# The opening of a two-block kernel: first weights in halves on ScalarE's queue, products of zeros ahead, constants in two parts, and a bank for the fifth tile

## The chip, the cores and the metric

The kernel runs on one core of a Trainium2 chip. The metric is the device time of one execution in microseconds: 1484.77 us as the median of three runs (1482.9 to 1485.26).

A core has TensorE for matrix products, VectorE (DVE), ScalarE (ACT) and GpSimd (POOL) for elementwise work, and SyncE, which here only issues transfers. Each engine runs its own instructions in order, and they wait for each other through semaphores.

## The reference

The reference computes two transformer blocks one after the other on x of 512 tokens by 1024 features, in float32. The first one's mixer is a linear recurrence (RWKV-7) beside a cross attention to 256 memory tokens; the change touches its beginning alone:

```python
kv = rms_norm(mem, mem_norm_g) @ w_mem_kv
h = rms_norm(x, norm_mix_g)
proj = h @ w_in                       # 1024 -> 2816 features
slab = token_shift(proj[..., :2560], mu)   # z + (z_prev - z) * mu
q_mem = proj[..., 2560:]
r, k, v, wd, ad, gd = split(slab)
log_w = -softplus(-(w0 + tanh(wd) @ w2)) - 0.5
a = sigmoid(a0 + ad @ a2)
g = sigmoid(gd) @ g2
...                                   # delta rule over 512 steps, 12 heads
x = x + concat([mix, mem_out]) @ w_out
x = x + square(relu(rms_norm(x) @ w_ff1)) @ w_ff2
# second block: neighbourhood and sliding window attention, gated; then a SwiGLU
```

## The kernel before

Activations lie with features on the partitions, so a product of weights and x gives a tile of 128 features by 512 tokens. Float32 accuracy is had from three fast products: a weight matrix and x are each split into a high part (`Whi`, `Hhi`: rounded to the fast format by ScalarE) and a low part (`Wlo`, `Hlo`: the remainder, subtracted by VectorE), and a *block* of 128 input features is Whi·Hhi, Wlo·Hhi, Whi·Hlo (`mm3`, called from L1089's `mm`). A tile of eight blocks is therefore 24 products of 128x512.

Weights come in *units* of 128x1024 (512 KB), one unit for one tile. SyncE loads a unit into one of three sets (`Wraw`, set 0 to 2, and set 3 once), ScalarE casts it (`split` in the scalar program, L2135), VectorE subtracts (L1685). A set may be overwritten by the next cast only when the tile that used it has ended (`of_unit`), so ScalarE waits for TensorE there.

`make_plan` writes one list of steps. Each engine walks through it and takes the steps that are its own, so a step's place in the list is its place on every engine. In the beginning the list brings x in eight pieces of 128 features (`xload`, `x`), and four tiles grow side by side, one block each per piece (`firsts`: wa, gd and two slabs, on units 0 to 3, sets 0 to 3). The norm of x is applied after the product. For its factor ScalarE squares and sums the rows of x (`row`, four of 128 tokens, L2150), takes the root (L2167), VectorE inverts it and spreads it (L1719, L1722, into `acc`), TensorE turns it by a transposing product (`rs`, L1203), and VectorE copies it to `RS` (L1732). Only then can VectorE read the four tiles out of their banks (L1742), after which ScalarE and VectorE do the token shift (L2200, L1819). Next come the fifth tile (unit 4, set 0), the two small products of the decay and rate (on `WA`, `w2s`), and the two tiles of memory queries (units 5 and 6, sets 1 and 2), then the memory projections (x 256 columns).

Accumulators are eight banks: two that tiles take in turn (`D`), five handed out round robin (`M`, where a tile may have its `own`), and one more (`OB`). Constants (`C`, 1794 columns) come in one transfer, needed first for the root's epsilon and the identity of the transposes.

## Time and profile before

| | |
|---|---|
| median of three runs | 1484.77 us |
| the profiled execution, its own time | 1485.25 us |
| its span, first to last instruction | 1483.5 us |
| TensorE, products busy | 1446.6 us, 98% |
| VectorE busy | 794.9 us, 54% |
| ScalarE busy | 555.4 us, 37% |
| GpSimd busy | 225.9 us, 15% |
| mean rate of transfers | 88 GB/s (331 in the first fortieth of the span) |

The span lies 1.75 us under the execution's own time. Busy shares are means over the span; matrix products are pipelined, and the ends of the rows are modelled, so the distance between starts says more than the duration that a row gives. "Idle before" in brackets is how long the engine had nothing, with what ended that.

### The profile page before, as it was taken

To read this page: it belongs to the slowest core of one execution; us is meant where nothing else is said; L and a number is where in the kernel's file an instruction comes from. 1 tells how busy PE (TensorE), PEld (TensorE's weight loads), DVE (VectorE), ACT (ScalarE), POOL (GpSimd) and SP (SyncE) were. 2 spreads that over 40 slices of the span, in tenths; PEclk is the share of its full clock that TensorE was granted. 3 is DMA by queue.
4 is the path that set the end of the run, shared out by engine and by line. 5 is a ranking of instruction groups with operands and counts; after the bars stand their busy time and mean duration, and the time that the engine had idled before them with its cause. 6 is when DMAs were issued, how large, how long until landed. Compare 5 with 4: busy or idle time off the path is not lost.

```text
span 1483.5 us, 26651 instructions
## 1 busy us (share of the span) xinstructions
PE 1446.6 (98%) x11374; PEld 1157.1 (78%) x11374; DVE 794.9 (54%) x1266; ACT 555.4 (37%) x942; POOL 225.9 (15%) x161
## 2 busy tenths in 40 slices
PE   7999999989999999999999999999999999999999
PEld 6877777666888888888888866767788888888887
DVE  5665676764563544536643457587554443443343
ACT  6544534552422221212532356555343222232221
POOL 0233333301200000000110001322112210220120
PEclk9999999999999999999999999999999999999999
DMA  8311111201323233332222232221232332333222
GB/s 331 114 30 46 31 31 45 74 3 59 99 86 102 97 100 93 106 93 92 94 91 86 81 111 79 89 68 58 86 99 93 101 104 87 100 97 103 85 86 99
DMA packets 39334, 130.89 MB, mean 88 GB/s; under 512 B 4272, under 2 KB 5296, under 8 KB 39216
## 3 DMA queue, kind: packets, MB, share of 16 engines
q1 hardware_dynamic: 39216, 129.18, 27.3%
q8 instruction: 90, 1.47, 0.4%
q14 instruction: 28, 0.23, 0.0%
HBM read 127.07 MB, written 2.10 MB: 87 GB/s over the span
## 4 chain that ended last, share of the span: by engine, by line
PE 87%; DVE 4%; issue 2%; ACT 2%; POOLq 0%; POOL 0%; DVEq 0%; ACTq 0%
PE bank L1089 85%; PE bank L1489 1%; PE bank L1203 1%; DVE slab L1819 0%; ACT kbr L2382 0%; ACT slab L2351 0%; DVE T L1924 0%; ACT Whi L2135 0%; PE bank L1279 0%; DVE Wlo L1685 0%; PE bank L1446 0%; DVE AR L1869 0%; DVE AR L1865 0%; DVE Xi L1931 0%; DVE ta L1868 0%
## 5 line engine op out<-in xcount | busy, mean ns | idle before, releaser
L1089 PE MATMUL bank<-Hhi,Whi 128*128 128x512 f32 x912 | 371.2, 407 | 8.7 <-DVE Wlo L1685 8.1
L1089 PE MATMUL bank<-Hlo,Whi 128*128 128x512 f32 x912 | 357.5, 392 | 0.0
L1089 PE MATMUL bank<-Hhi,Wlo 128*128 128x512 f32 x912 | 357.4, 392 | 0.0
L2135 ACT CAST Whi<-Wraw 128x1024 fp32r<-128x1024 f32 (+1 forms) x216 | 223.8, 1037 | 197.2 <-PE bank L1089 194.8
L1685 DVE TENSOR_TENSOR Wlo<-Wraw,Whi 128x1024 fp32r<-128x1024 f32 (+1 forms) x180 | 230.4, 1280 | 123.3 <-ACT Whi L2135 123.2
L1089 PE MATMUL bank<-Uhi,Whi 128*128 128x512 f32 x736 | 289.3, 393 | 1.6 <-DVE tmpb L1788 1.3
L1089 PE MATMUL bank<-Ulo,Whi 128*128 128x512 f32 x736 | 286.5, 389 | 0.0
L1089 PE MATMUL bank<-Uhi,Wlo 128*128 128x512 f32 x736 | 286.5, 389 | 0.0
L1089 PEld LDWEIGHTS bank<-Hhi,Whi 128*128 128x128 f32 x912 | 172.1, 189 | 56.8 <-issue 12.6
L1089 PEld LDWEIGHTS bank<-Hlo,Whi 128*128 128x128 f32 x912 | 172.2, 189 | 37.2
L1089 PEld LDWEIGHTS bank<-Hhi,Wlo 128*128 128x128 f32 x912 | 172.5, 189 | 33.0 <-issue 1.2
L1089 PEld LDWEIGHTS bank<-Uhi,Whi 128*128 128x128 f32 x736 | 138.1, 188 | 34.9 <-issue 3.8
L1089 PEld LDWEIGHTS bank<-Ulo,Whi 128*128 128x128 f32 x736 | 138.2, 188 | 28.9
L1089 PEld LDWEIGHTS bank<-Uhi,Wlo 128*128 128x128 f32 x736 | 138.2, 188 | 28.0 <-issue 0.2
L2463 POOL TENSOR_TENSOR Wlo<-Wraw,Whi 128x1024 fp32r<-128x1024 f32 x36 | 86.1, 2390 | 332.2 <-ACT Whi L2135 331.5
L1767 DVE TENSOR_TENSOR X<-X,bank 128x512 f32<-128x512 f32 x72 | 49.4, 686 | 138.2 <-PE bank L1089 138.1
L2471 POOL TENSOR_TENSOR accb<-accb,tmpb 128x512 f32<-128x512 f32 x14 | 18.9, 1352 | 375.9 <-ACT tmpb L2250 375.9
L2210 ACT CAST Uhi<-tmpb 128x512 fp32r<-128x512 f32 x32 | 19.9, 622 | 127.5 <-DVE tmpb L1776 127.5
L2476 POOL TENSOR_TENSOR qa<-qa 128x512 f32<-128x512 f32 x22 | 28.4, 1293 | 196.4 <-ACT qa L2220 196.4
L2224 ACT CAST Hhi<-qa 128x512 fp32r<-128x512 f32 x22 | 13.7, 622 | 114.6 <-POOL qa L2481 114.6
L2392 ACT ACTIVATE sr<-sr,st 128x256 f32<-128x256 f32 (+1 forms) x64 | 33.7, 528 | 34.7 <-DVE st L2060 20.4
L2077 DVE COPY pT<-bank 128x512 f32<-128x512 f32 (+2 forms) x48 | 25.3, 554 | 34.2 <-PE bank L1489 34.2
(292 smaller groups left out, 1556.4 us busy)
## 6 DMA issues: line engine op xcount, KB each, us to landing
Wraw<-in_wts SPq DMA_DIRECT2D x208, 512.0 KB, 3.5
bA<-in_biasA SPq DMA_DIRECT2D x12, 256.0 KB, 2.7
Wraw<-in_wts SPq DMA_DIRECT2D x8, 384.0 KB, 3.1
x<-in_xT SPq DMA_DIRECT2D x8, 256.0 KB, 4.5
x_rows<-in_xN SPq DMA_DIRECT2D x2, 1024.0 KB, 8.1
X<-in_xT SPq DMA_DIRECT2D x2, 1024.0 KB, 6.6
out<-X SPq DMA_DIRECT2D x8, 256.0 KB, 2.0
bB<-in_biasB SPq DMA_DIRECT2D x4, 384.0 KB, 3.0
```

Source lines behind the costliest of these rows:

```text
L1089: return e.matmul(o, lhsT, rhs, start=start, stop=stop, skip_group_check=True)
L1203: p = e.transpose(b[:, 128 * j:128 * j + 128], sq[:, 128 * j:128 * j + 128], c("ident"))
L1489: p = e.transpose(o, sr[n % 3][:, x:x + 128], c("ident"))
L1685: e.tensor_tensor(Wsp[k][1][:, 0:width], Wraw[k][:, 0:width], Wsp[k][0][:, 0:width].bitcast(F), ALU.subtract).then_inc(S["wlo"])
L1767: e.tensor_tensor(y, y, z, ALU.add).then_inc(S["evict"])
L2077: e.tensor_copy(pT[n % 2][:, width * i:width * i + wide], MB[plan.M.at["at", n, i]][:, 0:wide]).then_inc(S["at_out"])
L2135: e.copy(Wsp[k][0][:, 0:width], Wraw[k][:, 0:width]).then_inc(S["whi"])
L2210: e.copy(Uhi[:, x.key[1], :], tmp_of(("raw", t))[:]).then_inc(S["ffhi"])
L2392: p = e.activation(part, part, ACT.Exp, scale=1.0, bias=x[:, 2 + i:3 + i], accum_out=x[:, 4 + i:5 + i])
L2463: done(e.tensor_tensor(Wsp[k][1][:, 0:width], Wraw[k][:, 0:width], Wsp[k][0][:, 0:width].bitcast(F), ALU.subtract), "wlo_pool")
L2471: done(e.tensor_tensor(accb[:], accb[:], tmp_of(("sqr", *x.key))[:], ALU.add), "sq_add")
L2476: done(e.tensor_tensor(z[:], z[:], s[:], ALU.mult), "sig")
```

## The change

It touches the beginning alone; from the memory projections on, all engines have the same instructions in the same order as before.

- Unit 0's load leaves SyncE's queue. ScalarE issues it in two halves of 512 columns as its first instructions, casts each half by itself, and VectorE subtracts each half by itself.
- The very first block waits for its operands one by one and is written in the order Whi·Hhi, Whi·Hlo, Wlo·Hhi.
- VectorE sets a buffer (`km`) to zero, and TensorE multiplies it by itself four times (float32, 256 columns) ahead of everything.
- The constants come in two transfers (528 and 1280 columns with 14 of padding), later than before; the memory's second half is loaded, cast and split later.
- The fifth tile has its own bank. Its first four blocks stand ahead of the turning of the norm's rows. Unit 4 is loaded and cast earlier in the list: ahead of the last two row squares.
- Some semaphores are merged, and counts shifted by one.

On ScalarE, between the memory's splits and the load of the table for tanh, the rows were these (`x_rows` are the row squares, `st` the root, `Whi_62` the cast into set 0, `memHhi` the memory's high parts):

```order
L2156 ACTIVATE memHhi<-memX,V 128x256 [waits s_mem1]
L2156 ACTIVATE memHhi<-memX,V 128x256 x3
L2150 ACTIVATE x_rows,mst<-x_rows 128x1024 [waits s_xrows0]
L2150 ACTIVATE x_rows,mst<-x_rows 128x1024
L2150 ACTIVATE x_rows,mst<-x_rows 128x1024 [waits s_xrows1]
L2150 ACTIVATE x_rows,mst<-x_rows 128x1024
L2255 ACTIVATE spare<-C 128x1 [waits s_C]
L2167 ACTIVATE st_53<-mst,C 128x8 [waits s_xrow]
L2135 CAST Whi_62<-Wraw_59 128x1024 [waits s_tile,s_win0]
L2255 ACT_TABLE_LOAD
```

and they are now:

```order
L2212 ACTIVATE x_rows,mst<-x_rows 128x1024 [waits s_xrows0]
L2212 ACTIVATE x_rows,mst<-x_rows 128x1024
L2197 CAST Whi_62<-Wraw_59 128x1024 [waits s_tile,s_win0]
L2212 ACTIVATE x_rows,mst<-x_rows 128x1024 [waits s_xrows1]
L2212 ACTIVATE x_rows,mst<-x_rows 128x1024
L2317 ACTIVATE spare<-C 128x1 [waits s_C]
L2229 ACTIVATE st_53<-mst,C 128x8 [waits s_row]
L2218 ACTIVATE memHhi<-memX,V 128x256 [waits s_mem1]
L2218 ACTIVATE memHhi<-memX,V 128x256 x3
L2317 ACT_TABLE_LOAD
```

The cast, which waits for a tile to end, has moved ahead of two row squares and of the root; four of the memory's splits have moved behind it.

On TensorE, where the side-by-side tiles end (bank 2 and 3 are the two slabs, `C,acc` the turning of the norm's rows), there stood:

```order
L1089 MATMUL bank2<-Hhi_55,Wlo2_67 128x512
L1089 MATMUL bank2<-Hlo_56,Whi2_66 128x512
L1203 MATMUL bank4<-C_49,acc_100 128x128 [waits s_wide]
L1203 MATMUL bank4<-C_49,acc_100 128x128 x3
L1089 MATMUL bank3<-Hhi_55,Whi3_127 128x512
L1089 MATMUL bank3<-Hhi_55,Wlo3_128 128x512
```

and now, with the twelve products of the fifth tile's first four blocks shown by their first three:

```order
L1102 MATMUL bank3<-Hhi_55,Wlo3_128 128x512
L1102 MATMUL bank3<-Hlo_56,Whi3_127 128x512
L1102 MATMUL bank4<-Hhi_55,Whi0_62 128x512 [waits s_wlo]
L1102 MATMUL bank4<-Hhi_55,Wlo0_63 128x512
L1102 MATMUL bank4<-Hlo_56,Whi0_62 128x512
...
L1239 MATMUL bank5<-C_49,acc_100 128x128 [waits s_wide]
L1239 MATMUL bank5<-C_49,acc_100 128x128 x3
L1102 MATMUL bank3<-Hhi_55,Whi3_127 128x512
```

The turning moved behind four blocks of the fifth tile, which wait for unit 4's split. The diff, without the hunks that only rename or recount semaphores:

```diff
--- before
+++ after
@@ -20,6 +20,8 @@
 LEVELS = (1, 2, 4, 8, 16, 32)
+WARM = 4
+AHEAD = 2
 DECAY = 0.6065306597126334
@@ -28,9 +30,9 @@
 
-CONSTS = [("bd64", 128), ("mean", 128), ("ident", 128), ("cent", 128),
+CONSTS = [("bd64", 128), ("mean", 128), ("ident", 128), ("cent", 128), ("rmseps", 1), ("gneps", 1), ("pad", 14),
           ("mneg", 64), ("mpos", 64), ("inclneg", 64), ("inclpos", 64),
-          ("level", 64 * 5), ("first", 64), ("firstt", 64), ("same", 64), ("scan", 512), ("rmseps", 1), ("gneps", 1)]
+          ("level", 64 * 5), ("first", 64), ("firstt", 64), ("same", 64), ("scan", 512)]
 VECS = [("gmem", 8), ("gmix", 8), ("gffn", 8), ("mu", 20), ("w0", 6), ("a0", 6), ("kk", 6),
...
@@ -392,26 +395,36 @@
 
-        if i == 1:
-            step("cload")
-        elif i in (2, 3):
-            step("memload", i - 2)
+        if i == 2:
+            step("memload", 0)
         if i == 3:
-            for j in range(2):
-                step("rowload", "x", j)
+            step("rowload", "x", 0)
+            loads(5)
+            step("rowload", "x", 1)
+            step("cload", 0)
+            step("memload", 1)
             loads(6)
+            step("cload", 1)
             step("gateload")
         if i == 7:
-            for j in range(8):
+            for j in range(4):
                 mem_token(j)
-            for j in range(4):
+            for j in range(2):
+                step("row", "x", j)
+            splits(5)
+            for j in range(2, 4):
                 step("row", "x", j)
             next(first_norm)
+            for j in range(4, 8):
+                mem_token(j)
 
         for g, n in zip(firsts, ((1, 0, 0, 0), (1, 2, 2, 0), (1, 1, 1, 0))[i] if i < 3 else (1, 1, 1, i < 7)):
             for _ in range(n):
                 next(g)
-    splits(5)
+    first_values = couples(tile("slab", (0, 2), ("rw", 12), "x", range(8), own=True))
+    next(firsts[3])
+    for _ in range(AHEAD):
+        next(first_values)
     run(first_norm)
@@ -593,8 +606,8 @@
     def values_and_queries():
-        v = projection(0, 2)
-        yield from itertools.islice(v, 4)
+        v = first_values
+        yield from itertools.islice(v, 4 - AHEAD)
         t = read_out(v)
...
@@ -1122,10 +1135,33 @@
 
+        def first_block():
+
+            whi, wlo = Wsp[0]
+            o = bank_of(0)[:, 0:T]
+            w.wait_ge(S["whi"], 1)
+            w.wait_ge(S["xhi"], 1)
+            mm(o, whi[:, 0:128], Hhi1[:, 0, :], True, False)
+            w.wait_ge(S["Hlo"], 1)
+            mm(o, whi[:, 0:128], Hlo[:, 0, :], False, False)
+            w.wait_ge(S["wlo"], 1)
+            mm(o, wlo[:, 0:128], Hhi1[:, 0, :], False, False)
+
+        def warm_up():
+
+            w.wait_ge(S["setup"], 1)
+            for i in range(WARM):
+                mm(OB[:, 0:256], km[:, 0, 0:128], km[:, 1, :], True, True)
+
         def weight_block(t, i):
+            if t == 0 and i == 0:
+                first_block()
+                return
             x = tiles[t]
             hi, lo = acts(x.ver)
-            if i == 0:
+            if x.unit == 0:
+                w.wait_ge(S["wlo"], 1 if i < 4 else 2)
+            elif i == 0:
                 w.wait_ge(*lo_of(x.unit))
...
@@ -1306,6 +1342,7 @@
         def turn_a(p):
+            w.wait_ge(S["C_rest"], 16)
             crossed("na", (p,), 64, lambda h, ch, half: AR[p % 2][64 * h:64 * h + 64, 0, 64 * ch:64 * ch + 64],
...
@@ -1532,6 +1569,7 @@
                  "mv": mem_values, "as": scores, "at": turn_weights, "av": weighted, "vbt": turn_vb}
+        warm_up()
         for kind, *key in plan.steps:
@@ -1665,6 +1703,7 @@
         def setup():
+            e.memset(km[:], 0.0).then_inc(S["setup"])
             w.wait_ge(S["V"], 16)
@@ -1676,10 +1715,22 @@
 
+        def first_split():
+
+            raw, hi, lo = Wraw[0], Wsp[0][0], Wsp[0][1]
+            w.wait_ge(S["whi"], 1)
+            e.tensor_tensor(lo[:, 0:512], raw[:, 0:512], hi[:, 0:512].bitcast(F), ALU.subtract).then_inc(S["wlo"])
+            w.wait_ge(S["whi"], 2)
+            e.tensor_tensor(lo[:, 512:1024], raw[:, 512:1024], hi[:, 512:1024].bitcast(F),
+                            ALU.subtract).then_inc(S["wlo"])
+
         def split(u):
+            if u == 0:
+                first_split()
+                return
             lo, n = lo_of(u)
             if plan.numbers[("lo", u)] == "wlo":
-                w.wait_ge(S["whi"], u + 1)
+                w.wait_ge(S["whi"], u + 2)
                 width = units[u][1]
...
@@ -2123,7 +2175,17 @@
 
+        def first_split():
+
+            w.wait_ge(S["win_a"], 16)
+            e.copy(Wsp[0][0][:, 0:512], Wraw[0][:, 0:512]).then_inc(S["whi"])
+            w.wait_ge(S["win0"], 16)
+            e.copy(Wsp[0][0][:, 512:1024], Wraw[0][:, 512:1024]).then_inc(S["whi"])
+
         def split(u):
+            if u == 0:
+                first_split()
+                return
             k, before = sets.at[u], sets.before[u]
...
@@ -2420,6 +2482,12 @@
 
+        def first_unit():
+
+            e.dma_start(Wraw[0][:, 0:512], wts[0, :, 0:512]).then_inc(S["win_a"], 16)
+            e.dma_start(Wraw[0][:, 512:1024], wts[0, :, 512:1024]).then_inc(S["win0"], 16)
+
+        first_unit()
         w.wait_ge(S["zero"], 1)
...
@@ -2558,7 +2626,8 @@
             width = units[u][1]
-            e.dma_start(Wraw[k][:, 0:width], wts[u, :, 0:width]).then_inc(S[f"win{k}"], 16)
+            if u:
+                e.dma_start(Wraw[k][:, 0:width], wts[u, :, 0:width]).then_inc(S[f"win{k}"], 16)
 
@@ -2569,16 +2638,17 @@
 
-        def constants_in():
-            e.dma_start(C[:], cst).then_inc(S["C"], 16)
+        def constants_in(i):
+            a, z = ((0, C_FIRST), (C_FIRST, NCST))[i]
+            e.dma_start(C[:, a:z], cst[:, a:z]).then_inc(S[("C", "C_rest")[i]], 16)
 
         def mem_in(i):
             e.dma_start(memX[:, 4 * i:4 * i + 4, :],
                         memT[4 * i:4 * i + 4].rearrange("k p n -> p k n")).then_inc(S[f"mem{i}"], 16)
 
         def gates_in():
-            e.dma_start(w2s[:], w2a2).then_inc(S["w2"], 16)
-            e.dma_start(g2s[:], g2).then_inc(S["g2"], 16)
+            e.dma_start(w2s[:], w2a2).then_inc(S["w2g2"], 16)
+            e.dma_start(g2s[:], g2).then_inc(S["w2g2"], 16)
             e.dma_start(mem_rows[:], memN.rearrange("k p n -> p k n")).then_inc(S["memrows"], 16)
...
```

## Rows read from the trace of the kernel before

**Rows 1.** The page, the chain that ended last, by engine.

```profile
PE 87%; DVE 4%; issue 2%; ACT 2%; POOLq 0%; POOL 0%; DVEq 0%; ACTq 0%
```

**Rows 2.** Waits of TensorE, 0 to 66 us: total us, times, longest.

```profile
PE bank L1089 <- DVE Wlo L1685: 8.1, 1, 8.1
PE bank L1089 <- ACT x L2204: 0.9, 2, 0.6
```

**Rows 3.** Timeline of TensorE, opening: start, us, engine, line, operands, count.

```profile
8.07 0.79 PE L1089 MATMUL bank<-Hhi,Whi 128*128 128x512 f32 x1 [8.07 <-DVE Wlo L1685]
...
12.51 0.63 PE L1089 MATMUL bank<-Hhi,Wlo 128*128 128x512 f32 x1
12.94 0.45 PE L1089 MATMUL bank<-Hlo,Whi 128*128 128x512 f32 x1
...
13.70 0.39 PE L1089 MATMUL bank<-Hlo,Whi 128*128 128x512 f32 x1
...
69.86 1.12 PE L1089 MATMUL bank<-ftmp,C 128*128 128x512 f32 x2
```

**Rows 4.** Windows: stretch, busy by engine (x), granted clock, DMA share, GB/s.

```profile
2.00:3.00 1.00, 0.00 (x0) 0.00 (x0) 0.48 (x7) 0.23 (x2) 0.00 (x0) 1.00 0.67 138
3.00:4.00 1.00, 0.00 (x0) 0.00 (x0) 0.18 (x3) 0.01 (x1) 0.00 (x0) 1.00 1.22 334
...
8.10:10.00 1.90, 1.90 (x5) 1.51 (x6) 1.22 (x2) 1.53 (x2) 0.00 (x0) 1.00 1.02 399
```

**Rows 5.** Timeline of ScalarE, opening to 37 us.

```profile
4.00 0.72 ACT L2141 ACTIVATE Hhi<-x,V 128x512 fp32r<-128x512 f32 x1 [1.75 <-DMA x<-in_xT]
...
8.28 1.05 ACT L2135 CAST Whi<-Wraw 128x1024 fp32r<-128x1024 f32 x1 [0.90 <-DMA Wraw<-in_wts]
...
25.97 1.04 ACT L2150 ACTIVATE x_rows<-x_rows 128x1024 f32<-128x1024 f32 x1
...
27.01 0.19 ACT L2255 ACTIVATE spare<-C 128x1 f32<-128x1 f32 x1
...
28.48 1.05 ACT L2135 CAST Whi<-Wraw 128x1024 fp32r<-128x1024 f32 x1 [1.04 <-PE bank L1089]
...
36.65 1.03 ACT L2135 CAST Whi<-Wraw 128x1024 fp32r<-128x1024 f32 x1
```

**Rows 6.** Timeline of VectorE, opening to 38 us.

```profile
6.79 1.23 DVE L1685 TENSOR_TENSOR Wlo<-Wraw,Whi 128x1024 fp32r<-128x1024 f32 x1 [1.29 <-ACT Whi L2135]
...
9.36 2.45 DVE L1685 TENSOR_TENSOR Wlo<-Wraw,Whi 128x1024 fp32r<-128x1024 f32 x2 [0.68 <-ACT Whi L2135]
...
19.79 3.25 DVE L1696 SCALAR_TENSOR_TENSOR memHlo<-memX,V,memHhi 128x256 fp32r<-128x256 f32 x8
...
27.70 0.43 DVE L1722 COPY acc<-st 128x512 f32<-128x512 f32 x1
...
30.70 0.68 DVE L1732 COPY RS<-bank 128x512 f32<-128x512 f32 x1
...
37.71 1.23 DVE L1685 TENSOR_TENSOR Wlo<-Wraw,Whi 128x1024 fp32r<-128x1024 f32 x1 [1.07 <-ACT Whi L2135]
```

**Rows 7.** Timeline of TensorE, 28 to 54 us.

```profile
28.00 0.39 PE L1089 MATMUL bank<-Hlo,Whi 128*128 128x512 f32 x1
...
29.59 0.60 PE L1203 MATMUL bank<-C,acc 128*128 128x128 f32 x4
...
36.94 1.13 PE L1089 MATMUL bank<-WA,w2s 64*128 64x512 f32 x4
...
39.48 0.40 PE L1089 MATMUL bank<-Hhi,Whi 128*128 128x512 f32 x1
...
50.68 1.16 PE L1089 MATMUL bank<-C,x 128*128 128x128 f32 x8 [0.59 <-ACT x L2204]
...
53.50 0.28 PE L1089 MATMUL bank<-memHhi,Whi 128*128 128x256 f32 x1
```

**Rows 8.** Timeline of SyncE, opening: the issue of the first weights.

```profile
1.63 0.42 SPq L2561 DMA_DIRECT2D Wraw<-in_wts  x1
```

More of the change, by code:

```diff
@@ L47 @@
 C_AT, NCST = offsets(CONSTS)
+C_FIRST = C_AT["mneg"][0]
 V_AT, NVEC = offsets(VECS)
@@ L958, in block_program @@
     assert top[0] <= nc.sbuf_usable_end, top[0]
-    old, old_end = (C_AT_BYTES + 4 * C_AT[n][0] for n in ("mneg", "rmseps"))
+    old, old_end = (C_AT_BYTES + 4 * n for n in (C_FIRST, NCST))
     sr.append(sb_at("sr2", [128, 768], F, old))
@@ L998, in block_program @@
     S = {n: nc.alloc_semaphore("s_" + n) for n in (
-        "V C w2 g2 mem0 mem1 memrows xrows0 xrows1 X0 X1 xin0 xin1 xin2 xin3 win0 win1 win2 win3 win4 bias0 bias1 bias2 out "
+        "V C C_rest w2g2 win_a mem0 mem1 memrows xrows0 xrows1 X0 X1 xin0 xin1 xin2 xin3 win0 win1 win2 win3 win4 bias0 bias1 bias2 out "
         "whi wlo wlo_pool Hlo Ulo mlo umem memhi mixhi ffhi bothhi uphi uhi "
@@ L1009, in block_program @@
         "ms_out mt_out va_act va_dve as_out at_out vbt_out "
-        "setup zero gd dve wide xhi xrow mrow mhi hsq lora shift_a shift sgp tap cum kf0 exp pc kksq bt rk ar bb "
+        "setup zero gd dve wide xhi row mhi hsq lora shift_a shift sgp tap cum kf0 exp pc kksq bt rk ar bb "
         "bk x0 y0 ai zsq bonus mmax mrec pn hkb amax aexp arec an sqr gated gact gsig sig act resq "
@@ L1082, in lo_of @@
         kind = plan.numbers[("lo", u)]
-        return S[kind], N(kind, u)
+        return S[kind], N(kind, u) + (kind == "wlo")
     def tensor_program(e):
@@ L1219, in decay @@
         def decay(p):
-            w.wait_ge(S["w2"], 16)
+            w.wait_ge(S["w2g2"], 32)
             w.wait_ge(S["lora"], 1)
@@ L1426, in gate_rows @@
         def gate_rows(p):
-            w.wait_ge(S["g2"], 16)
+            w.wait_ge(S["w2g2"], 32)
             w.wait_ge(S["gd"], 1)
@@ L1835, in cumulate @@
             w.wait_ge(S["sgp"], p + 1)
+            w.wait_ge(S["C_rest"], 16)
             e.tensor_tensor_scan(sg[:], c("scan"), sg[:], 0.0, ALU.mult, ALU.add).then_inc(S["cum"])
@@ L1990, in head_rows @@
             w.wait_ge(S["hn"], N("hn", t))
-            w.wait_ge(S["setup"], 1)
+            w.wait_ge(S["setup"], 2)
             if x.kind == "km":
@@ L2150, in row_squares @@
             e.activation(rows_, rows_, ACT.Square, scale=1.0,
-                         accum_out=row_sums[name][:, j:j + 1]).then_inc(S[name + "row"])
+                         accum_out=row_sums[name][:, j:j + 1]).then_inc(S["row"])
         def mem_token(i):
@@ L2164, in root @@
             if kind in ("x", "m"):
-                w.wait_ge(S[kind + "row"], n // 128)
+                w.wait_ge(S["row"], 4 if kind == "x" else 6)
                 one = row_sums[kind].unsqueeze(2).broadcast_to([128, n // 128, 2])
@@ L2189, in evict @@
                 dst, z, j = shifted(t)
-                w.wait_ge(S["setup"], 1)
+                w.wait_ge(S["setup"], 2)
                 if x.kind == "slab" and x.key[0]:
@@ L2260, in decay @@
             w.wait_ge(S["sg"], p + 1)
-            w.wait_ge(S["setup"], 1)
+            w.wait_ge(S["setup"], 2)
             e.activation(sg[:], MB[plan.M.at["sg", p]][:], ACT.Tanh, scale=0.5,
@@ L2275, in keys @@
             w.wait_ge(S["tap"], p + 1)
-            w.wait_ge(S["setup"], 1)
+            w.wait_ge(S["setup"], 2)
             w.wait_ge(S["sk"], p)
@@ L2459, in split @@
             if plan.numbers[("lo", u)] == "wlo_pool":
-                w.wait_ge(S["whi"], u + 1)
+                w.wait_ge(S["whi"], u + 2)
                 turn()
```

## Prediction, before the changed kernel was run

> **What bounds the kernel now.** I read the page first: the chain of waits that ends last is TensorE's for 87% [rows 1]. A change elsewhere counts only where it shortens or lengthens a TensorE wait. So the second view was TensorE's waits up to 66 us. The two longest entries are 8.1 us before its first product, for the low half of the first weights, and 0.9 us in two waits for ScalarE [rows 2]. From 8.07 us to 49.7 us it never stands still. Third came the timelines of the opening, and last the same timelines at 28 to 40 us, where the change reorders work.
>
> [...] First, the first product starts at 8.07 us. [...] The engine had stood still for 8.07 us before, and then worked without a pause for 4.9 us until the spacing fell. The granted clock of the windows reads 1.00 even there [rows 4], so it is the spacing that tells the level.
>
> **The change part by part.** I go in four steps: start of the dense stream, the chain that it releases, the stretch after, and the edits that cost nothing.
>
> *Step 1, the start.* The first weights leave SyncE's queue for ScalarE's, in halves, and the first block needs only the high halves to begin. ScalarE's high half of x took 0.72 us from 4.00 [rows 5]; a 512-wide cast is about half of the 1.05 us of a 1024-wide one [rows 5], 0.55; so the first product may start near 5.4 us instead of 8.07. But the order then wants the second weight tile after six products, and its path is not shortened by any edit except the transfer: landing at 8.28 (the cast starts there, and its wait ends on the transfer), split at 9.36 and 1.28 us from the split's start to the product, as 6.79 to 8.07 at the first tile [rows 3, 5, 6]. That is 8.28 + 1.08 + 1.28 = 10.64. What matters is how much earlier that transfer lands. The core moved 138 GB/s from 2 to 3 us and 334 from 3 to 4, against 399 later [rows 4]: only the first 3 us are not full. Two queues issuing at once can fill at most about (399 - 138) + (399 - 334) = 326 KB of that, 0.8 us at 399; the least is nothing, if the two share what one had. I take 0.5 (nearer to the filled end, since SyncE also issues everything behind the first weights one slot earlier). So the dense stream starts at 10.14 us.
>
> The products of zeros: the trace has no such product that cold. The nearest row is the fp32 product of 128x512, two passes in 1.12 us at the fast level (69.86) [rows 3]; 256 columns are half, 0.56, and at the slow level 1.12; four are 2.2 to 4.5 us. The zeroing memset needs well under 1 us, so they lie between about 1.3 and 5.8 us, where the engine stood still: free, or up to 0.4 us off the first block, which has 10.14 - 5.8 us to spare. What they may buy is the fast level at 10.14.
>
> If it is fast: the tile that frees weight set 0 ends 71 products after the dense stream's first. At 0.227 us that is 16.1 us, so its last product starts at 26.26 instead of 28.00 [rows 3, 7]. The opening's gain at this point is G = 1.74 us.
>
> *Step 2, the chain that is released.* Write c for the moment at which ScalarE casts the fifth unit's weights (set 0): 28.48 before, 0.48 behind that last product [rows 5, 7], so 26.74 now. Before, the sums of squares of x were all done by then (27.01), TensorE turned their rows at 29.59 and VectorE copied them at 30.70, that is c + 2.22 [rows 5 to 7]. Now the cast stands ahead of two of the four row squares, and TensorE takes four blocks of the fifth tile ahead of the turning. ScalarE's side: cast 1.05, two squares of 1.04, and 1.12 from the small step at 27.01 to the end of VectorE's spread copy at 28.13 give c + 4.3 [rows 5, 6]. TensorE's side: the fifth tile's split is ready at c + 1.08 + 1.28 = c + 2.36 (three blocks after the freeing tile are over at c + 1.8, so it waits 0.6), four blocks are 12 x 0.227 = 2.72, and the turned rows are readable 0.60 to 1.11 later (29.59 x4 took 0.60; the copy at 30.70 is the upper end, as VectorE was still splitting). I take 0.66: c + 5.74. TensorE's side ends last, and VectorE's four memory splits that now stand ahead of the copy end a little sooner: the root is over at c + 3.5, then four high parts and the last low part at 0.41 each (3.25 for eight) make c + 5.5 [rows 6]. So the copy comes 5.74 - 2.22 = 3.52 us later against c, and 3.52 - 1.74 = 1.78 us later on the clock: 32.48.
>
> From the copy on, VectorE and ScalarE hand five evictions and shifts to each other in the old order. The cast of set 1 starts 5.95 after the copy (36.65) and its split 7.01 after (37.71) [rows 5, 6]; nothing in this stretch waited for TensorE, so it moves as a block. The split is then ready for TensorE at 32.48 + 7.01 + 1.28 = 40.77. TensorE gets there sooner: turning 0.36, nine and twelve products of 0.227, and 1.1 for the two small products (36.94, four passes) after c + 5.08 = 31.82 make 38.1 [rows 7]. It waits 2.7 us. Before it began set 1 at 39.48 with the split ready at 38.99: half a microsecond of cover, which is gone. Set 1 starts 40.77 - 39.48 = 1.29 us later than before. In general: 3.03 - G.
>
> *Step 3, from set 1 to the memory projections (53.50).* The same products stand here in a little other order. The trace has one wait of 0.59 in the stretch, at 50.68, for ScalarE [rows 7]. Now the key rows' turning stands last and waits for a table load and root that are queued behind more of ScalarE's casts. If TensorE is alone the limit, 0.6 is won; if ScalarE's queue is, up to 1 is lost. I take -0.1. From there on the order is the old one, and the lag stays: +1.2 us.
>
> *Edits at nothing.* Constants in two parts and the memory's second half later: both land in a stretch of full transfers some microseconds before their first use, and c + 3.1 (the first constant needed) is 29.8. If they were late, each microsecond would add one to the chain of step 2. The merged semaphores change no order. The own bank takes away a wait for an eviction that did not bind. The two DMA issues on ScalarE are 0.42 us each by SyncE's row [rows 8]; ScalarE stood idle for 1.75 us before x landed at 4.00 [rows 5], which covers both. If that cover were gone, the delay would still end before the second weights land.
>
> Sum against the profiled execution (span 1483.5, its own time 1485.25): +1.2 gives 1486.45. The median of the three runs is 1484.77, so by it 1485.97; I say 1486.0.
>
> **The rivals.**
>
> A. The gain stays. If set 1's split is ready when TensorE comes, the result is step 1 alone: -1.7 at G = 1.74 and -2.6 at most (transfer 0.8 earlier, first stretch 0.6 of step 3), so 1483.0. For it: the four blocks of the fifth tile are work put ahead of the turning, which is cover. Against it: TensorE's work up to set 1 has the same length as before, while the chain from the cast grew by 3.5. It needs 2.7 us that I do not see.
>
> B. The slow level is back when the dense stream starts. Between the first blocks and 10.14 TensorE has six products to do in over 4 us, and in step 2 it stands 2.7 us. A stretch like that of the trace, 11 products spaced 0.43 instead of 0.227 [rows 3], costs 2.2 us: G = -0.5, and the result is 3.03 + 0.5 - 0.1 = +3.4, 1488.2. It decides from 9 such products on (G below 0). [...]
>
> C. The second queue brings nothing: the transfers share the rate and the second weights land at 8.28 as before. Then G = 1.24 and the result +1.7, 1486.5. [...] The trace shows the rate short of full before 3 us, so there is room that a second queue can fill, and the forecast takes part of it.
>
> **How the numbers follow.** Forecast 0.50, A 0.15, B 0.22, C 0.13. Change of less than 0.2%, 3.0 us, is what a measurement here cannot tell from none: the three runs alone spread by 2.4. Forecast and C lie inside it; A passes it only with a good run (0.07 in all); B passes it most of the time (0.16, and 0.03 from the forecast's tail). So faster 0.07, same 0.74, slower 0.19. The range takes A's 1483 less a little scatter, and B's 1488.2 with some: 1482.8 to 1489.0. Forecast and C alone would be 1484.5 to 1487.5.
>
> **What would show it.** In the changed trace: first real product between 5.0 and 6.2 us; second weight tile's first product at 9.8 to 10.6, spaced 0.23 from there (0.43: rival B); the fifth unit's cast at 26.2 to 27.3; TensorE waiting about 0.6 us for that split; the copy of the turned rows at 32 to 33; and a wait of 2 to 3.5 us for set 1's split at about 38 us, which the old trace doesn't have. If that wait is under 0.5 us, step 2 is wrong; if it is there and the total still falls, G was mis-sized.

## Result and profile after

The changed kernel takes 1486.60 us as the median of 15 runs (1484.60 to 1489.32), the kernel before 1483.50 us on the same chip (15 runs, 1481.54 to 1485.66): a ratio of 1.0024, 95% interval 1.0017 to 1.0031. The medians are 3.1 us apart, and the interval is 2.5 to 4.6 us. The forecast was 1486.0, but as 1.2 above before. The median came close partly because the three runs of before that I started from were 1.3 us higher than fifteen are. The ratios here and below leave out one execution of 3644 us, of the kernel without zeros in the next section, whose median counts it. The profiled execution has a span of 1484.2 us and took 1486.00.

The chain of the page is still TensorE's for 87% [rows 1]:

```profile
PE 87%; DVE 5%; issue 2%; ACT 2%; POOLq 0%; POOL 0%; ACTq 0%; DVEq 0%
```

The waits of TensorE from 0 to 66 us (total us, times, longest), which answer to [rows 2]:

```profile
PE bank L1102 <- DVE Wlo L1736: 2.9, 2, 2.5
PE bank L1102 <- DVE km L1706: 1.5, 1, 1.5
PE bank L1102 <- ACT Whi L2181: 1.4, 1, 1.4
PE bank L1239 <- DVE VD L1768: 0.6, 1, 0.6
PE bank L1102 <- DVE Hlo L1742: 0.5, 1, 0.5
PE bank L1102 <- ACT x L2266: 0.2, 1, 0.2
```

The 8.1 us ahead of the first product are gone. In their place stand 1.5 before the zeros, 1.4 and 0.5 among the first blocks, and a new 2.5 for a low half of weights. Where that one is, the timeline of TensorE tells. First the opening, beside [rows 3] (start, us, engine, line, operands):

```profile
1.45 3.78 PE L1102 MATMUL bank<-km 128*128 128x256 f32 x8 [1.45 <-DVE km L1706]
6.60 0.80 PE L1102 MATMUL bank<-Hhi,Whi 128*128 128x512 f32 x1 [1.37 <-ACT Whi L2181]
...
8.75 0.80 PE L1102 MATMUL bank<-Hhi,Whi 128*128 128x512 f32 x1 [0.47 <-DVE Hlo L1742]
...
10.19 0.63 PE L1102 MATMUL bank<-Hhi,Whi 128*128 128x512 f32 x1
10.62 0.63 PE L1102 MATMUL bank<-Hhi,Wlo 128*128 128x512 f32 x1
...
13.18 0.49 PE L1102 MATMUL bank<-Hhi,Wlo 128*128 128x512 f32 x1
13.50 0.40 PE L1102 MATMUL bank<-Hlo,Whi 128*128 128x512 f32 x1
```

The second weight tile starts at 10.19, and its products are 0.43 us apart until 13.18. This spacing of 512-wide products is called the slow level here, and 0.227 us, measured before from 13.70 to 28.00 [rows 3, 7], the fast one. The slow level lasts about as long into the program as before, where it ended at 12.94. The same engine from 30 us on, beside [rows 7]:

```profile
30.67 0.50 PE L1102 MATMUL bank<-Hhi,Whi 128*128 128x512 f32 x1 [0.41 <-DVE Wlo L1736]
...
33.53 0.60 PE L1239 MATMUL bank<-C,acc 128*128 128x128 f32 x4
...
42.45 0.50 PE L1102 MATMUL bank<-Hhi,Whi 128*128 128x512 f32 x1 [2.47 <-DVE Wlo L1736]
...
56.21 0.63 PE L1239 MATMUL bank<-C,ftmp 128*128 128x128 f32 x4 [0.63 <-DVE VD L1768]
56.59 0.36 PE L1102 MATMUL bank<-memHhi,Whi 128*128 128x256 f32 x1
```

The turning (33.53) was at 29.59, set 1's first product (42.45) at 39.48, and the memory projections (56.59) began at 53.50: 2.97 us late, then 3.09. ScalarE, beside [rows 5]:

```profile
5.32 0.72 ACT L2203 ACTIVATE Hhi<-x,V 128x512 fp32r<-128x512 f32 x1 [2.15 <-DMA x<-in_xT]
...
28.31 1.05 ACT L2197 CAST Whi<-Wraw 128x1024 fp32r<-128x1024 f32 x1 [5.56 <-PE bank L1102]
...
40.12 1.03 ACT L2197 CAST Whi<-Wraw 128x1024 fp32r<-128x1024 f32 x1
```

VectorE in the same stretch, beside [rows 6]:

```profile
29.39 1.23 DVE L1736 TENSOR_TENSOR Wlo<-Wraw,Whi 128x1024 fp32r<-128x1024 f32 x1 [8.69 <-ACT Whi L2197]
...
32.05 0.43 DVE L1773 COPY acc<-st 128x512 f32<-128x512 f32 x1
32.40 1.67 DVE L1747 SCALAR_TENSOR_TENSOR memHlo<-memX,V,memHhi 128x256 fp32r<-128x256 f32 x4
34.17 0.69 DVE L1783 COPY RS<-bank 128x512 f32<-128x512 f32 x1
...
41.18 1.23 DVE L1736 TENSOR_TENSOR Wlo<-Wraw,Whi 128x1024 fp32r<-128x1024 f32 x1 [1.06 <-ACT Whi L2197]
```

The cast of the fifth unit (28.31) came 0.17 us sooner than before, the copy of the turned rows (34.17) 3.47 later. The transfers, by windows beside [rows 4] (the last number is GB/s):

```profile
2.00:3.00 1.00, 1.00 (x4) 0.78 (x3) 0.00 (x0) 0.99 (x2) 0.00 (x0) 1.00 0.80 186
3.00:4.00 1.00, 1.00 (x4) 0.82 (x3) 0.35 (x5) 0.16 (x1) 0.00 (x0) 1.00 0.95 320
```

The issue of the first half on ScalarE's queue, beside [rows 8]:

```profile
0.73 0.41 ACTq L2487 DMA_DIRECT2D Wraw<-in_wts  x1
```

From 2 to 3 us the core moved 186 GB/s where it had moved 138, and from 3 to 4 us 320 where it had moved 334; ScalarE issues the first half at 0.73, where SyncE had issued the whole at 1.63. The two halves landed at 3.99 and 5.48 (the whole at 5.69 before) and the second weights at 7.63 instead of 8.26. The vectors, however, landed at 3.62 instead of 2.49 and the first piece of x at 5.23 instead of 3.91.

### The profile page after: what moved, and what is told of

It reads as the page before. It is cut to its first block, busy times and chain, and to the rows that moved or that the text cites. A ratio compares the mean times of both kernels' runs of the same rounds, so it can differ in the third digit from the quotient of the medians.

```text
span 1484.2 us, 26671 instructions
## 1 busy us (share of the span) xinstructions
PE 1449.1 (98%) x11382; PEld 1157.5 (78%) x11382; DVE 795.1 (54%) x1268; ACT 555.1 (37%) x943; POOL 224.3 (15%) x161
## 4 chain that ended last, share of the span: by engine, by line
PE 87%; DVE 5%; issue 2%; ACT 2%; POOLq 0%; POOL 0%; ACTq 0%; DVEq 0%
PE bank L1102 85%; PE bank L1526 1%; PE bank L1239 0%; DVE slab L1870 0%; PE bank L1483 0%; ACT kbr L2444 0%; DVE T L1976 0%; ACT Whi L2197 0%; PE bank L1315 0%; DVE Wlo L1736 0%; DVE AR L1921 0%; DVE AR L1917 0%; DVE Xi L1983 0%; ACT slab L2413 0%; DVE ta L1920 0%
## 5 line engine op out<-in xcount | busy, mean ns | idle before, releaser
L2544 POOL TENSOR_TENSOR qa<-qa 128x512 f32<-128x512 f32 x22 | 28.5, 1294 | 196.8 <-ACT qa L2282 196.8
```

The lines of the kernel that those rows point to most:

```text
L2544: done(e.tensor_tensor(z[:], z[:], s[:], ALU.mult), "sig")
```

## Experiments

I call the lag of a kernel how much later than in the kernel before an instruction that both have starts. It is read between 60 and 290 us, since farther on the profiled executions differ by the stretches in which the granted clock fell (last section). Each kernel ran beside the kernel before, whose medians were 1483.35, 1483.16, 1483.12 and 1483.47 us in the four sessions.

**The order undone.** Steps for row squares, cast and fifth tile as before the change, its loads kept:

```diff
-            for j in range(4):
+            for j in range(8):
                 mem_token(j)
-            for j in range(2):
-                step("row", "x", j)
-            splits(5)
-            for j in range(2, 4):
+            for j in range(4):
                 step("row", "x", j)
             next(first_norm)
-            for j in range(4, 8):
-                mem_token(j)
...
-    for _ in range(AHEAD):
-        next(first_values)
+    splits(5)
```

> The changed kernel with its edits at the very start (halves, first block, zeros, constants in two parts) but with the old order of the row squares, the root, the fifth unit's cast and the fifth tile. Theory (the lag is the chain cast, split, four blocks, turning, copy): the copy of the turned rows comes 2.2 us behind the fifth unit's cast instead of 5.9, the first product on weight set 1 at about 39.3 us instead of 42.45, no wait of 2.5 us there, and the time 0.2 us under before, 3.3 us under the changed kernel. Rival (the lag comes from the later transfers of constants, memory and weights, or from the two queues): set 1 still begins at 42 us or later and the time stays about 3 us over before.

1487.86 us, ratio 1.0032 (1.0020 to 1.0044): a miss. It was no clean undoing. ScalarE now stood before all four row squares, waiting for the memory's second half, which the new order of loads brings later, in its timeline:

```profile
26.52 1.71 ACT L2210 ACTIVATE memHhi<-memX,V 128x256 fp32r<-128x256 f32 x4 [6.45 <-DMA memX<-in_memT]
```

So the root came late, and TensorE waited 3.4 us for it, in its timeline:

```profile
33.48 0.66 PE L1231 MATMUL bank<-C,acc 128*128 128x128 f32 x4 [3.38 <-DVE acc L1765]
```

The order of the loads and that of the steps belong together.

**The order alone**, put into the kernel before (the lines above the other way round, nothing of the start):

> The kernel before with nothing but the new order of row squares, root, fifth unit's cast and fifth tile. Theory: the start is that of before (first product at 8.07 us, cast at 28.5 us), the copy of the turned rows 5.8 us behind the cast, set 1 at 42.5 us, and the time 3.0 us over before. Rival (the new order is harmless, the lag belongs to the transfers or the start): set 1 at 39.5 us and the time of before.

1486.39 us, 1.0022 (1.0013 to 1.0031), as the theory had it. The cast came at 28.53, the copy of the rows at 34.39 (5.86 behind it), and set 1 waited:

```profile
42.68 0.50 PE L1098 MATMUL bank<-Hhi,Whi 128*128 128x512 f32 x1 [2.45 <-DVE Wlo L1694]
```

**The start alone**: the start's edits with the old order of steps and of loads.

```diff
-        if i == 2:
-            step("memload", 0)
+        if i == 1:
+            step("cload", 0)
+            step("cload", 1)
+        elif i in (2, 3):
+            step("memload", i - 2)
         if i == 3:
-            step("rowload", "x", 0)
-            loads(5)
-            step("rowload", "x", 1)
...
+            for j in range(2):
+                step("rowload", "x", j)
             loads(6)
```

> All of the start's edits (first weights in halves on ScalarE's queue, first block by operand, products of zeros, constants in two parts), with the order of the row squares, the cast, the fifth tile and of every later load as before the change. Theory (the start's edits are worth the 0.17 us that the cast of the fifth unit gained, and the whole loss is the new order's): first product 6.5, cast of the fifth unit at 28.2 to 28.4, copy of the turned rows 2.2 behind it (30.5), set 1 begins at 39.2 to 39.4 with no wait over 0.3 us for its split; time 0.1 to 0.3 us below the kernel before (1483.1 on a chip where before is 1483.35). It would also say that the 3.4 us wait of the first undoing came from its load order. Rival (the later landings of the first vectors and of x, from queues that now share, cost something of their own): set 1 over 1 us late, time 1 to 3 us above before.

1483.25 us, 1.0002 (0.9994 to 1.0011). Cast 28.61, copy 30.84, no wait for set 1, and up to 60 us no longer wait behind the first blocks than the 0.54 for the key rows (0.59 in before). The lag is +0.10 to +0.15 up to 200 us (0.3 to 0.4 at 245 to 280), not the small gain expected: in this execution the spacing fell only at 14.04. So the order is the loss (+3.0 between the medians), and the start is worth nothing, in trace and in time.

**No zeros** (`WARM = 0`), and **ones instead of zeros** (`e.memset(km[:], 1.0)`):

> The changed kernel without the four products of zeros. Theory (they bought nothing: the products after 6.6 us were spaced 0.43 us until 13.3 us all the same): the spacing falls to 0.23 us between 12 and 15 us again, set 1 begins within 0.5 us of 42.45, the time is that of the changed kernel within 0.5 us. Rival (they shortened the slow stretch that follows): the spacing falls 2 us later or more and the time grows by 1 us.

> The changed kernel with its four early products made of ones instead of zeros; nothing else. Theory A (what counts is that TensorE is busy, and four products in 1.45 to 5.23 us with the pause behind them are too little): the spacing falls at about 13 us as with zeros, same time. Theory B (zeros do not count as work): the spacing falls to 0.23 us well before 11 us, the fifth unit's cast comes 1 to 1.5 us sooner than 28.31, and the time is 1 to 1.5 us under the changed kernel.

1488.01 us, 1.0028 (1.0018 to 1.0038), and 1486.05 us, 1.0018 (1.0008 to 1.0028). With none, the slow spacing ended at 13.05; with four of ones at 13.98; with four of zeros at 13.2 in the changed kernel, and between 12.7 and 14.9 in the other kernels with four. Set 1 waited 2.45 and 2.48 us. The median without zeros is 1.4 us above the changed kernel's, where 0.5 was expected; the intervals overlap, and in the trace the lag is a little smaller (2.97 against 3.2 at 90 us). So no gain of the eight passes shows, and the values in them are not the reason.

**The cast back** behind all four squares and the root, the four blocks still ahead of the turning:

```diff
-            for j in range(2):
-                step("row", "x", j)
-            splits(5)
-            for j in range(2, 4):
+            for j in range(4):
                 step("row", "x", j)
             next(first_norm)
             for j in range(4, 8):
                 mem_token(j)
+            splits(5)
```

> The changed kernel, with the cast of the fifth unit back behind all four row squares, the root and the memory's last tokens; the four blocks of the fifth tile still stand ahead of the turning of the rows on TensorE. Theory (TensorE's side of the chain ends last: split, four blocks, turning, copy): the root is ready in time, and yet the copy comes 5.6 to 6.0 us behind the cast and set 1 waits 2.4 us or more; time 3 us or more above before. Rival (it was the cast among ScalarE's row squares that delayed the root): copy 2.2 behind the cast, no wait for set 1, time within 0.5 us of before.

1486.37 us, 1.0022 (1.0012 to 1.0032), as the theory had it. VectorE's spread copy was over at 27.75, yet TensorE turned it at 34.27, behind the four blocks:

```profile
34.27 0.60 PE L1237 MATMUL bank<-C,acc 128*128 128x128 f32 x4
...
43.19 0.50 PE L1100 MATMUL bank<-Hhi,Whi 128*128 128x512 f32 x1 [2.45 <-DVE Wlo L1734]
```

**No blocks ahead** (`AHEAD = 0`), the cast early as in the changed kernel:

> The changed kernel, with the cast of the fifth unit as early as in it, but no blocks of the fifth tile ahead of the turning (AHEAD 0). By the prediction's step 2, ScalarE's and VectorE's side then ends last: copy of the turned rows 4.3 to 5.2 us behind the cast instead of 5.86, so 0.7 to 1.5 us sooner; TensorE waits 2.0 to 3.5 us before the turning for the copied root, and then hardly at set 1; time 1.5 to 2.5 us above before. Rival (the four blocks are the whole loss): copy 2.2 to 3 behind the cast, time within 0.5 us of before.

1486.75 us, 1.0020 (1.0011 to 1.0030), that is 1.6 to 4.4 us above before where 1.5 to 2.5 was expected. TensorE waited for the root, as expected, and not at set 1; but the copy came at 33.63, 5.67 behind the cast (27.96), not 4.3 to 5.2. VectorE, with the fifth unit's split and the memory splits:

```profile
31.70 0.43 DVE L1773 COPY acc<-st 128x512 f32<-128x512 f32 x1
32.05 1.67 DVE L1747 SCALAR_TENSOR_TENSOR memHlo<-memX,V,memHhi 128x256 fp32r<-128x256 f32 x4
33.63 0.68 DVE L1783 COPY RS<-bank 128x512 f32<-128x512 f32 x1
```

The spread copy ended at c + 4.2, where step 2 had c + 4.3, and then the four memory splits stood before the copy: the c + 5.5 that step 2 gives for VectorE, which I forgot in this expectation. The two sides end 0.2 us apart, so taking off one of them gives nothing back.

**Ten products of zeros** in the changed kernel (`WARM = 10`), so that TensorE works up to its first block:

> The changed kernel with 10 products of zeros (20 passes) instead of 4, so that TensorE has no pause between them and the first block. Theory (the slow level stayed because TensorE stood still between the zeros and the dense stream, so my forecast's own condition wasn't met): the spacing falls to 0.227 before 9 us, the zeros end by 8.5 to 9.5, second weight tile's first product at 10.2 to 10.6 at the fast level, cast of the fifth unit at 26.6 to 27.2, set 1's wait about 2.4 as before, lag from set 1 on 1.3 to 2.0; time 1.3 to 1.8 us above before, so 1.3 to 1.8 below the changed kernel. Rival (the start's work doesn't set the level, or products of zeros don't count): spacing 0.43 until about 13, first product late at about 10, cast at 28.3 or later, time 3 us or more above before.

1486.31 us, 1.0020 (1.0011 to 1.0029). The trace did what was expected up to set 1. The zeros' spacing halved at 4.85 us and stayed so through the first blocks:

```profile
1.45 6.16 PE L1102 MATMUL bank<-km 128*128 128x256 f32 x20 [1.45 <-DVE km L1706]
...
10.44 0.50 PE L1102 MATMUL bank<-Hhi,Whi 128*128 128x512 f32 x1 [0.23 <-DVE Wlo L1736]
10.78 0.39 PE L1102 MATMUL bank<-Hhi,Wlo 128*128 128x512 f32 x1
```

VectorE's copy of the turned rows in the same kernel:

```profile
33.01 0.69 DVE L1783 COPY RS<-bank 128x512 f32<-128x512 f32 x1
```

And TensorE's first product of set 1 behind it:

```profile
41.30 0.50 PE L1102 MATMUL bank<-Hhi,Whi 128*128 128x512 f32 x1 [2.46 <-DVE Wlo L1736]
```

The cast came at 27.15, so G = 1.33; the copy 5.86 behind it; set 1 at 41.30, which is 1.82 behind before, where 3.03 - G gives 1.70. Behind that wait the clock fell (a window of 42.3 to 45.5; the column ahead of the DMA share is the granted clock), and the lag grew to 2.47:

```profile
42.30:45.50 3.20, 3.20 (x9) 2.45 (x9) 1.16 (x2) 2.76 (x5) 1.22 (x2) 0.50 0.45 159
```

The time doesn't show the gain: the interval (1.6 to 4.3 us above before) just touches what was expected (1.3 to 1.8) and holds the changed kernel's 3.1 too.

**The start with ten zeros** and the old order, **the kernel before with eleven zeros** and nothing else, and **one queue**, the first again with the halves issued by SyncE. The first and third change the start alone by the two lines shown; the second adds the memset, `warm_up` and `WARM = 11` to the kernel before; the third also moves the two issues:

```diff
-WARM = 4
+WARM = 10
...
-        first_unit()
...
+            else:
+                e.dma_start(Wraw[0][:, 0:512], wts[0, :, 0:512]).then_inc(S["win_a"], 16)
+                e.dma_start(Wraw[0][:, 512:1024], wts[0, :, 512:1024]).then_inc(S["win0"], 16)
```

> The start's edits with 10 products of zeros instead of 4, and the old order of the row squares, the cast, the fifth tile and the loads (the start alone, made to reach the fast level). Theory (by the trace of the changed kernel with 10 products of zeros the level rises at about 4.7 us and stays; the loss was the order's): second weight tile's first product at 10.2 to 10.6 spaced 0.227, cast of the fifth unit at 26.9 to 27.3, copy of the turned rows 2.2 behind it, set 1's split ready at copy + 8.28 = 37.4 to 37.8, TensorE there at 38.1 to 38.4, so no wait over 0.3 us; lag -1.1 to -1.4 from set 1 on, time 1.1 to 1.4 us below before, about 1481.9 where before is 1483.2. Rival (what is won at the start is given back later, by another wait or by the clock): lag at 120 us between -0.5 and +1, time within 0.6 us of before.

> The kernel before, with nothing added but the zeroing memset and 11 products of zeros ahead of its first product (no second queue, no halves, old order). Theory (the level is what the start can win, the earlier first product isn't): level up at about 4.7 us, zeros end by 7.9, first product at 8.1 spaced 0.227, a new wait of about 1 us for the second weights (ready at 10.64 by the old transfer), cast of the fifth unit at 27.0 to 27.3, lag -1.1 to -1.4 at 120 us, time 1.1 to 1.4 us below before. Rival (the level falls back in the wait for the second weights, or the second queue was needed): spacing 0.43 again behind 10.6, cast at 28 or later, time within 0.5 us of before.

> As the start with 10 products of zeros and the old order, but the two halves of the first weights are issued by SyncE, behind the vectors and the first token, so that all loads are in one queue again. Theory (the second queue takes its share from the vectors and from x, and gives the weights behind it what SyncE no longer issues): vectors landed at 2.5, first token at 3.9, halves at 4.8 and 5.7, second weights at 8.1 to 8.4 (7.5 to 7.8 with two queues); first product by the zeros' end at 7.2 to 7.3, second weight tile at 10.4 to 10.8, cast of the fifth unit within 0.3 us of the two queues'; time within 0.5 us of it. Rival (the second queue is needed): second weight tile and cast 0.6 us or more later.

1483.86 us, 1.0000 (0.9990 to 1.0009); 1481.50 us, 0.9994 (0.9986 to 1.0002); 1483.27 us, 1.0005 (0.9996 to 1.0014). In all three the fast level was there (from 5.87, 6.20 and 7.85 us) before the second weight tile (10.42, 10.67 and 11.03 us), and in none of the profiled executions did the gain stay: lags +0.1, +0.15 and +0.7. For the kernel before with zeros the times leave a small gain open: the interval runs from 2.1 us below before to 0.3 above. TensorE met a new wait at the turning. The kernel before with zeros, one line of TensorE's waits from 0 to 66 us:

```profile
PE bank L1210 <- DVE acc L1731: 0.9, 1, 0.9
```

Its third row square on ScalarE:

```profile
26.25 1.06 ACT L2159 ACTIVATE x_rows<-x_rows 128x1024 f32<-128x1024 f32 x1 [1.45 <-DMA x_rows<-in_xN]
```

And its transfers from 23 to 25 us (queue: packets, MB, share of 16 engines):

```profile
q1 hardware_dynamic: 223, 0.80, 99.6%
q8 instruction: 1, 0.02, 3.0%
```

The squares of x's last rows begin when those rows have landed: at 26.25 here, at 24.91 in before, where the spread copy (28.13) stood ready 1.46 us before TensorE turned it [rows 6, 7]. That was all the cover there was, and two things together used it up: TensorE came 1.1 sooner, and the rows came 1.3 later. By these rows the 1.1 alone would have fitted into the cover. In this kernel a piece of instructions (16 KB, one packet of 1.0 us on one transfer engine, at 23.61) was loaded among the rows, whose second half landed 3.6 us behind the first instead of 2.5; in before that packet came at 33.85, in the changed kernel at 28.15. With one queue (packet at 24.43) the halves also landed 3.6 apart. In the start with ten zeros both landed 1.7 later than in the start with four, and only 2.55 apart, with the packet (23.89) behind the first half's landing (23.61), so there the packet can't be the cause, and what is stays open. That the packet delays the rows is read from these rows, not tested.

One queue also settled what the second one does: vectors at 2.60 and first piece of x at 3.97 as in before, second weights at 8.64, against 8.03 with two. The second weight tile came 0.6 later, and so did the cast, as the rival said.

**Rows first**, to remove that bound: the changed kernel's loads, ten zeros, old order, and the memory's last four tokens behind the cast of set 1.

```diff
     splits(6)
     shift(held[3])
+    for j in range(4, 8):
+        mem_token(j)
```

> The changed kernel with 10 products of zeros, its own order of loads (x's rows ahead of the memory's second half), but the cast of the fifth unit behind the four row squares and the root, no blocks of the fifth tile ahead, and the memory's last four tokens only behind the cast of set 1. Theory (the start's gain was lost twice: with the old loads the rows of x land too late for an earlier turning, 24.5 to 26.2 us, and with the new order the cast and the four blocks stand ahead of it; with the rows first and the old order nothing is in its way): level up at 4.7 to 5.9 us, second weight tile at 10.2 to 10.5, row squares over by 26.8, cast of the fifth unit at 27.0 to 27.4, copy of the turned rows at 29.2 to 29.7, set 1's first product at 38.1 to 38.5 with no wait over 0.3 us, lag -1.0 to -1.3 at 120 us, time 1.0 to 1.3 us below before (1482.1 where before is 1483.1). Rival (the moved tokens or another wait take it back): a wait of over 0.5 us between 28 and 60 us that before does not have, lag at 120 us between -0.5 and +2, time not below before.

1485.20 us, 1.0006 (0.9997 to 1.0015): a miss. The rows landed at 26.0 again (packet at 23.87), TensorE waited 0.94 at the turning and reached set 1 at 39.30, only 0.18 sooner than before (38.1 to 38.5 was expected). Then the key rows came late; that the four tokens, which now stand in the queues of ScalarE and VectorE, are the reason is read from the order, not tested:

```profile
39.30 0.40 PE L1096 MATMUL bank<-Hhi,Whi 128*128 128x512 f32 x1
...
52.21 1.45 PE L1096 MATMUL bank<-C,x 128*128 128x128 f32 x8 [2.31 <-ACT x L2260]
```

By that wait the profiled execution was 1.5 us behind before, and behind it the granted clock was 0.50 from 53 to 56.3 us, so that its lag is 2.9 from 66 us on, above both expectations. The interval of the times is 0.4 below before to 2.2 above.

No version here is shown to beat the kernel before.

## Why the prediction was right, and which size was off

The sign, the place and the range held; the forecast itself did not come about by its own sum. What came about is rival B, and that 1486.0 lies only 0.6 below the median is luck: G was 1.57 short, and the start of the sum was 1.3 too high.

*Step 1, the start: the step that failed.* The forecast took the fast level at 10.14 us and G = 1.74. The transfer term came out in size: the second weights landed 0.63 sooner (0.5 taken), and their first product came at 10.19. Its reason did not: from 2 to 4 us, the stretch that was to be filled, the core moved 506 KB where it had moved 472, which is worth about 0.1 us at 399 GB/s by my estimate. What the rest comes from stays open, and so does part of the size: with the start of before the second weights landed at 7.84 to 8.29 in three kernels, with the second queue at 7.41 to 8.03 in ten. But the first real product came at 6.60, not near 5.4, because x landed 1.3 later (with one queue it landed at 3.97, as before): the second queue cost what stood first on the other one, which I had counted only for the weights behind. And the products of 10.19 were 0.43 apart until 13.18. The 0.227 us of the sum is the mean of the 63 distances from 13.70 to 28.00 in the trace before [rows 3, 7]. Counting from 10.19, the nine distances up to 13.74 took 3.55 us instead of 9 x 0.227 = 2.04, which costs 1.5 us; G came out as 28.48 - 28.31 = 0.17. That is rival B's outcome at about two thirds of its price (11 products, 2.2 us, G = -0.5 there). The ten zeros give the counterproof: with more products and no pause ahead of the first block the level was up at 4.85 and G was 1.33. Which of the two did it, the number or the missing pause, that run does not separate.

Rival B had the slow level back because TensorE has little to do between the first blocks and 10.14; that pauses bring it back was the author's assumption. In the changed kernel's own execution the zeros were 0.43 apart and the first blocks too, so the fast level did not show there; in two others with the same four zeros it had risen and fell back. The kernel without blocks ahead, TensorE's timeline:

```profile
6.62 0.50 PE L1102 MATMUL bank<-Hhi,Whi 128*128 128x512 f32 x1 [1.38 <-ACT Whi L2181]
6.95 0.44 PE L1102 MATMUL bank<-Hlo,Whi 128*128 128x512 f32 x1
...
10.55 0.63 PE L1102 MATMUL bank<-Hhi,Wlo 128*128 128x512 f32 x1
10.97 0.63 PE L1102 MATMUL bank<-Hlo,Whi 128*128 128x512 f32 x1
```

And two windows of it, with the granted clock ahead of the DMA share:

```profile
6.60:9.20 2.60, 1.71 (x5) 0.96 (x6) 2.60 (x5) 2.33 (x4) 0.00 (x0) 1.00 1.04 419
9.40:12.60 3.20, 3.20 (x8) 2.15 (x7) 3.05 (x4) 2.93 (x5) 0.00 (x0) 0.50 0.85 323
```

The first block starts with 0.33 us from product to product, the fast level, where the changed kernel has 0.60 (6.60 to 7.20); after a pause of 1.38 ahead of it and one of 0.77 behind it the granted clock is 0.50 from 9.4 on. So the slow level came back behind pauses here; but with ten zeros a pause of 0.77 left the fast one up (0.33 from 9.25 to 9.58), and no run here shows how long a pause has to be.

The trace before has falls behind pauses too: its granted clock went to 0.50 at 296.4, 337.3 and 876.6 us, behind or in pauses of 1.37, 1.22 and 1.90 us. The last one, in TensorE's timeline of the kernel before:

```profile
877.08 1.23 PE L1089 MATMUL bank<-ka,qa 64*128 64x256 f32 x4 [1.90 <-DVE sr L2047]
...
879.26 0.63 PE L1089 MATMUL bank<-Hlo,Whi 128*128 128x512 f32 x1
879.68 0.63 PE L1089 MATMUL bank<-Hhi,Whi 128*128 128x512 f32 x1
```

The products are 0.43 us apart again. Between the zeros and 10.14 the forecast's own plan had such pauses, so rival B could have been given more than 0.22 from rows that were there.

Rival C had the transfers share the rate. What was issued on SyncE's queue at the same time did land later: the vectors 1.13 and x 1.32 us. Rival C's conclusion, no gain for the second weights, is not borne out: 0.63 in the changed kernel, 8.03 with two queues against 8.64 with one, and about 0.4 between the means of the two groups above, whose ranges overlap.

*Step 2, the chain: right to a tenth.* Copy at c + 5.86 (5.74 forecast), cast of set 1 5.95 behind it (5.95), its split 7.01 behind it (7.01), wait 2.47 (2.7), set 1 at +2.97; by 3.03 - G it is +2.86. The 0.41 us wait for the fifth unit's split is the 0.6 of the text. TensorE's side and VectorE's ended together: the turning began 0.64 ahead of the copy, as in the kernel with the cast back, where VectorE stood free, and VectorE's memory splits were over at 34.07. The undoing in parts shows both sides: with the blocks ahead alone the copy is at c + 5.91, with the cast ahead alone at c + 5.67. Rival A is out: a wait of 2.45 to 2.48 for set 1 is there in every kernel with the whole new order.

*Step 3.* -0.1 was taken. The wait for the key rows fell from 0.59 to 0.2, but one of 0.63 came just ahead of the memory projections. The lag went from 2.97 to 3.09 there and to 3.29 at 200 us (the cast of 200.74 stands at 204.03), so about +0.3.

*Edits at nothing.* The constants, semaphores and the bank show no wait of their own. "Both land some microseconds before their first use" held.

*Sum:* 1.2 forecast, +1.57 for G, +0.1 in step 2, +0.4 in step 3 give 3.3 by the trace. By the times it is 3.1 between the medians, and the interval is 2.5 to 4.6.

## What to carry to other kernels

Price a gain at the start only down to the next engine that stands ready: here the spread root was ready 1.46 us ahead of TensorE, so no more than that could stay, and 1.3 of it went when the rows landed later. Work that an order puts ahead of a chain's link delays the chain by what TensorE or VectorE must finish first (here the copy moved from 2.2 to 5.9 us behind the cast), and taking back one of two such pieces gave nothing while the other ended within 0.2 us of it. Four warm-up products with a pause behind them bought nothing here; ten that ran into the real work brought the fast level (from 4.85 us) to the first blocks, and even that was not clear of the noise in the time.

## What the runs showed of the hardware

- The spacing of TensorE's products fell from 0.43 us to 0.22 (zeros of 256 columns) or 0.23 (real products of 512): among the zeros at 4.85, 5.31, 5.87, 6.20 and 7.85 us in five kernels that all worked without a pause from 1.45 on, and in the dense stream only at 12.7 to 14.9 in the six others that began at 1.45, which paused before 6.5 to 6.6; without zeros, in the changed kernel, it fell at 13.05.
- Behind a wait of TensorE of 2.3 to 3.4 us in the dense stream the granted clock fell to 0.50 in five executions (waits of 2.28, 2.31, 2.45, 2.46 and 3.38) and in four it didn't (2.45 to 2.48, among them the changed kernel's 2.47). In the kernel without blocks ahead it did, behind 2.28 us; eight products there, from 33.54 to 36.52, were spaced 0.43:

```profile
33.20:36.60 3.40, 3.40 (x10) 2.63 (x9) 3.10 (x6) 2.67 (x4) 0.00 (x0) 0.50 0.63 249
```

- Later in the program such falls come behind shorter pauses of TensorE, of 1.2 to 1.9 us, that both kernels have, and they differ between executions: the granted clock from 870 to 890 us is 0.83 in the profiled execution of before and 0.91 in that of the changed kernel, with the same pause of 1.90 in it. Across 290 to 350 us the lag went from 3.2 to 2.3, across 870 to 890 us from 2.1 to 0.75. That is why the spans of the profiled executions differ by 0.7 us, while the lag at 200 us is 3.29 and the medians differ by 3.1.

- The 16 KB piece of instructions is loaded sooner the more warm-up products there are: at 31.9 to 33.9 us in the three kernels without any, at 27.7 to 28.5 with four, at 23.6 to 24.4 with ten or eleven.
